# Two transformer blocks on one core: the second block's context norm and 24 context merge gates are computed among the expert pairs

## The reference

```python
def expert_choice_ffn(h, w_router, w_gate, w_up, w_down):
    cap = CAPACITY_FACTOR * n // N_EXPERTS            # 64 tokens for each of 16 experts
    aff = jax.nn.softmax((h @ w_router).astype(jnp.float32), axis=-1)
    gate, idx = lax.top_k(jnp.swapaxes(aff, 1, 2), cap)
    xe = h[bidx, idx]
    hid = jax.nn.silu(xe @ w_gate) * (xe @ w_up)      # per expert, 1024 x 1024 each
    ye = (hid @ w_down) * gate[..., None]
    return jnp.zeros_like(h).at[bidx, idx].add(ye)

def trunk_layer(x, xc, mod, mod_c, ..., with_ctx_out):      # second block
    z = split_columns_2((rmsnorm(x, pre_g) * (1 + scale) + shift) @ w_in)
    zc = split_columns_2((rmsnorm(xc, pre_g) * (1 + scale_c) + shift_c) @ w_in)
    ...
def merge_branches(zz, y_mla, y_pool, y_gla, w_bm, w_bp, w_bg, w_out):
    gates = jax.nn.sigmoid(zz['merge'])               # 3 x 1024 columns
    g_mla, g_pool, g_gla = jnp.split(gates, N_BRANCH, axis=-1)
    merged = g_mla * (y_mla @ w_bm) + g_pool * (y_pool @ w_bp) + g_gla * (y_gla @ w_bg)
    return merged @ w_out
```

## Time and profile before

| | |
|---|---|
| median of 3 runs | 2923.61 us (2909.93, 2923.61, 2923.92) |
| profiled execution, its own time | 2912.22 us |
| its span | 2910.3 us |
| PE busy | 2761.8 us (95%), 15104 matmuls |
| PEld busy | 2087.5 us (72%) |
| DVE, ACT, POOL busy | 1032.6, 911.5, 629.2 us |
| weights on SP's queue (q1) | 378.56 MB |
| mean granted TensorE clock | 0.981 |

### The profile page before, as it was taken

How to read it: one execution, slowest core, us unless ns; L and a number is a source line. 1 busy time by engine, 2 the same in 40 slices (tenths; PEclk the granted TensorE clock), 3 DMA queues, 4 the chain that set the end, 5 groups by cost and what they waited for, 6 DMA issues and landing times.

```text
span 2910.3 us, 36846 instructions
## 1 busy us (share of the span) xinstructions
PE 2761.8 (95%) x15104; PEld 2087.5 (72%) x15104; DVE 1032.6 (35%) x1485; ACT 911.5 (31%) x1379; POOL 629.2 (22%) x301
## 2 busy tenths in 40 slices
PE   6999899999989999999999999999998999898998
PEld 4856777788744433337899867999997878676886
DVE  3435512511351111113168443411135066645114
ACT  5222434422331111103333544311124243443223
POOL 1202021144410000001221102322222232105443
PEclk9999999999999999998999899999998999999999
DMA  6244032022369999994121202111123122103222
GB/s 259 73 175 180 1 132 87 30 102 96 136 277 420 422 422 422 422 422 194 62 90 59 80 1 95 59 62 69 58 102 131 58 103 85 44 27 112 101 87 101
DMA packets 65758, 426.19 MB, mean 146 GB/s; under 512 B 6928, under 2 KB 6928, under 8 KB 19280
## 3 DMA queue, kind: packets, MB, share of 16 engines
q1 hardware_dynamic: 52992, 378.56, 33.1%
q0 software_dynamic: 3664, 24.60, 2.2%
q10 hardware_dynamic: 8960, 20.97, 2.1%
HBM read 405.49 MB, written 17.04 MB: 145 GB/s over the span
## 4 chain that ended last, share of the span: by engine, by line
PE 77%; DMA 9%; DVE 6%; ACT 4%; issue 2%; POOL 1%; SPq 0%; ACTq 0%; DVEq 0%; POOLq 0%
PE psum L713 74%; DMA ring<-in_weights 5%; PE psum L716 4%; DMA late_slots<-in_weights 3%; DVE small L2362 1%; ACT arena L1824 1%; POOL weight_parts L3086 1%; ACT arena L1802 1%; ACT weight_parts L1748 0%; DVE arena L2825 0%; DVE hidden L2318 0%; DMA saved_residual<-residual 0%; DMA arena<-in_t_count 0%; DMA residual<-in_acts 0%; DVE hidden_low L2314 0%
## 5 line engine op out<-in xcount | busy, mean ns | idle before, releaser
L713 PE MATMUL psum<-hidden_high,weight_parts 128*128 128x384 f32 (+2 forms) x3296 | 863.7, 362 | 24.8 <-issue 7.3
L3086 POOL TENSOR_TENSOR weight_parts<-ring,weight_parts 128x1024 fp32r<-128x1024 f32 x224 | 559.7, 2500 | 1290.9 <-ACT weight_parts L1748 1290.8
L713 PEld LDWEIGHTS psum<-hidden_high,weight_parts 128*128 128x128 f32 x3296 | 601.2, 189 | 98.1 <-issue 17.3
L713 PE MATMUL psum<-hidden_low,weight_parts 128*128 128x384 f32 (+2 forms) x2160 | 650.9, 361 | 1.3 <-DVE merged_low L2430 0.7
L1748 ACT ACTIVATE weight_parts<-ring 128x1024 fp32r<-128x1024 f32 x224 | 236.9, 1059 | 1025.3 <-PE psum L713 989.2
L713 PE MATMUL psum<-arena 128*64 128x128 f32 (+8 forms) x2992 | 451.5, 359 | 11.7 <-DMA arena<-in_weights 6.5
L713 PEld LDWEIGHTS psum<-hidden_low,weight_parts 128*128 128x128 f32 x2160 | 399.6, 189 | 44.2 <-issue 2.5
L713 PEld LDWEIGHTS psum<-arena 128*64 128x64 f32 (+3 forms) x2992 | 255.4, 156 | 167.7 <-issue 129.3
L1802 ACT ACTIVATE arena<-psum 128x512 f32<-128x512 f32 (+2 forms) x202 | 147.8, 739 | 360.3 <-PE psum L713 341.7
L713 PE MATMUL psum<-arena_parts,weight_parts 128*128 128x512 f32 (+2 forms) x1140 | 250.4, 377 | 0.5 <-ACT arena L1802 0.5
L713 PEld LDWEIGHTS psum<-arena_parts,weight_parts 128*128 128x128 f32 x1140 | 211.0, 192 | 32.2 <-ACT arena L1802 0.9
(11 more groups left out here) (315 smaller groups left out, 2436.3 us busy)
## 6 DMA issues: line engine op xcount, KB each, us to landing
ring<-in_weights SPq DMA_DIRECT2D x260, 1024.0 KB, 6.7
late_slots<-in_weights SPq DMA_DIRECT2D x48, 1024.0 KB, 15.2
arena<-in_weights SPq DMA_DIRECT2D x48, 1024.0 KB, 17.3
spilled_projections<-arena ACTq DMA_DIRECT2D x14, 384.0 KB, 2.3
arena<-spilled_projections ACTq DMA_DIRECT2D x3, 1536.0 KB, 12.0
residual<-in_acts SPq DMA_DIRECT2D x4, 768.0 KB, 8.3
arena<-in_bias POOLq DMA_DIRECT2D x1, 3072.0 KB, 10.9
arena<-in_t_count POOLq DMA_DIRECT2D x2, 1536.0 KB, 10.5
```

What stands on the lines that cost most here:

```text
L713: return nc.tensor.matmul(o, lhsT, rhs, start=start, stop=stop)
L3086: G_.tensor_tensor(parts[:, i % 2, 1, :], tile_at(t), parts[:, i % 2, 0, :], ALU.subtract).then_inc(*E.sig("tile_split"))
```

## The change

The loop over pairs is replaced by eight pairs written out on PE, ACT and DVE. The context's sum of squares is taken in pair 0 after `exp_gate`, its root on ScalarE, its spreading on PE before `exp_down`, and its scaling, shift and parting (256 columns, 8 feature tiles) beside `exp_down` of pair 0. Pair 0 has no combine products. After `exp_down` of each of the pairs 0 to 5 stand four context gates: their tiles are 24 more tiles of the stream (12 units), each with a copy on ScalarE into `cHigh`, a subtraction in place on GpSimd, 24 matmuls of 256 columns, a sigmoid into one of three staging areas, and a transfer of 128 KB to memory from ScalarE's queue. In `merge` of layer 0 the gate tiles are still loaded and parted, but multiplied with the image only (24 matmuls of 512 columns); the context's gates come back from memory by a transfer that ScalarE starts after each sigmoid. The norm after the pairs covers the image only. `eHot` moves to the image half of `Hlo`, and SP's last loads into the eight slots follow the new count.

```diff
+CONTEXT_GATES = [(b, g) for f in range(0, KT, 2) for b in range(3) for g in (f, f + 1)]
+GATES_PER_PAIR = 4
...
+        for b, g in context_gates_after(j):
+            c0 = B2["merge"] + b * D + g * P
+            out.append((("cgate", b, g), "w_in_2", (0,), None, np.arange(c0, c0 + P)))
...
-    e1 = e0 + PAIRS * 3 * KT
+    e1 = e0 + PAIRS * 3 * KT + len(CONTEXT_GATES) // 2
...
-                        project_tile(("gate", *tags, b, g), ("gate", key, b, g), chunks)
+                        project_tile(("gate", *tags, b, g), ("gate", key, b, g), IMG)
...
+            def context_gate(b, g):
...
+                hi, lo = split(cHigh[i % 2], a=KT), split(tile_parts(n), a=KT)
+                pe.wait_ge(*E.next("context_weight_high"))
+                ps = group("cgate", b, g)
+                for k in range(KT):
+                    for m, h in enumerate((Hhi, Hlo)):
+                        ins = mm(ps[:, 0:CTX], hi[:, k, :], h[:, k, 0:CTX], k == 0 and m == 0, False)
...
+                pe.wait_ge(*E.next("context_weight_low"))
+                for k in range(KT):
+                    ins = mm(ps[:, 0:CTX], lo[:, k, :], Hhi[:, k, 0:CTX], False, k == KT - 1)
...
-                    if e and k:
+                    if j and e and k:
...
+                expert_product(tag, "exp_gate", j, eXE, after=combine_step)
+                if j == 0:
                     pe.wait_ge(*E.next("context_squares", KT))
                     ps = group("stat", "context")
...
+                if j == 0:
+                    pe.wait_ge(*E.next("context_parted", KT))
+                for b, g in context_gates_after(j):
+                    context_gate(b, g)
...
-            with pe.Fori(0, turns) as it:
...
-            pair("last", PAIRS - 1, PAIRS - 1, None)
+            for j in range(PAIRS):
+                pair(j)
...
-            spread(("pre", 0), 0, range(TT))
+            spread(("pre", 0), 0, range(2, TT))
...
+            def context_high(i):
+
+                n = context_tiles[i]
+                act.wait_ge(*arrived(n))
+                if i >= 2:
+                    act.wait_ge(*E.written("cgate", *CONTEXT_GATES[i - 2]))
+                act_(cHigh[i % 2], tile_at(n), ACT.Copy).then_inc(*E.sig("context_weight_high"))
+
+            def context_gate(i):
+
+                s = i % 3
+                if i >= 3:
+                    act.wait_ge(sem(f"context_spilled{s}"), 16 * (i // 3))
+                evac(("cgate", *CONTEXT_GATES[i]), cStage[s], n=CTX, func=ACT.Sigmoid)
+                act.wait_ge(*E.taken("cgate", *CONTEXT_GATES[i]))
+                act.dma_start(dram["context_gates"][i, :, :], cStage[s]).then_inc(sem(f"context_spilled{s}"), 16)
...
+                        evac(("gate", key, b, g), mSG[:, s, CTX:TOK], IMG, func=ACT.Sigmoid)
+                        if chunks is ALL:
+                            act.dma_start(mSG[:, s, 0:CTX], dram["context_gates"][CONTEXT_GATES.index((b, g)), :, :])\
+                                .then_inc(sem(f"context_gate{s}"), 16)
...
+                for i in gates[0:2]:
+                    context_high(i)
                 act.wait_ge(*E.next("gate_set"))
                 act.wait_ge(*E.written(tag, "exp_down"))
                 act_(eYhi, cols(tag, "exp_down"), ACT.Copy, scale=eGate).then_inc(*E.sig("expert_high"))
...
+                for i in gates:
+                    if i + 2 in gates:
+                        context_high(i + 2)
+                    context_gate(i)
...
-                shift_in(modB[l], 0, ALL)
+                shift_in(modB[l], 0, IMG if l == 0 else ALL)
...
+                            if chunks is ALL:
+                                dve.wait_ge(*E.next(f"context_gate{gate_slot(f, b, g)}", 16))
...
+            for i, n in enumerate(context_tiles):
+                pool.wait_ge(*E.next("context_weight_high"))
+                G_.tensor_tensor(tile_parts(n), tile_at(n), cHigh[i % 2], ALU.subtract)\
+                    .then_inc(*E.sig("context_weight_low"))
```

More of the change, by code:

```diff
@@ L1369, in pair @@
                         add_up(ps, k, cSq, range(2), C("ones")[:, 0:1])
+                expert_product(tag, "exp_up", j, eXE)
+                if not last:
+                    pe.wait_ge(*E.next("selected"))
+                    gather(tag, eSel)
                 pe.wait_ge(*E.next("expert_hidden"))
@@ L1411, in _ @@
             pe.wait_ge(*E.taken("first", "XT"))
-            while state["g"] % 3:
-                ps = group("pad", state["g"])
-                ins = mm(ps[:, 0:2], C("ident"), C("ident")[:, 0:2], True, True)
-                ins.then_inc(psum_full, 1)
-            assert state["owed"] == 1 and state["tile"] % 2 == 0, state
-            assert state["ended"] == state["tile"]
-            turns = PAIRS - 1
-            with pe.Fori(0, turns) as it:
-                E.begin(it, {"groups": 6, "slot": 2, "ring": 16 * 24 // (NSLOT + EXTRA), "expert_hidden": 1,
-                             "combined": 8, "hidden_first": 1, "selected": 1})
-                pair("loop", 0, it, it + 1)
-                assert state["owed"] == 1
-                E.end(turns)
-            state["g"] += 6 * (turns - 1)
-            state["tile"] += 48 * (turns - 1)
-            state["ended"] = state["tile"]
-            pair("last", PAIRS - 1, PAIRS - 1, None)
+            for j in range(PAIRS):
+                pair(j)
             keep_warm(5)
-            pe.wait_ge(*E.taken("last", "exp_down"))
+            pe.wait_ge(*E.taken(("pair", PAIRS - 1), "exp_down"))
             for q in range(4):
@@ L2061, in _ @@
                 act_(cSq[:, k, :], R3[:, k, 0:CTX], ACT.Square).then_inc(*E.sig("context_squares"))
-            pair("last", None)
+            for j in range(PAIRS):
+                pair(j)
+            for s in range(3):
+                act.wait_ge(sem(f"context_spilled{s}"), 16 * (len(CONTEXT_GATES) // 3))
             for k in range(KT):
@@ L2717, in pair @@
                     .then_inc(*E.read(tag, "exp_up"))
-                if not following:
-                    dve.wait_ge(*E.written("stat", "context"))
-                    ts_(var[:, 0:2], cols("stat", "context")[:, 0:2], 1.0 / D, EPS, ALU.mult, ALU.add)\
-                        .then_inc(*E.read("stat", "context"))
                 dve.wait_ge(*E.next("hidden_turned"))
@@ L2731, in pair @@
                     .then_inc(*E.read(tag, "exp_down"))
-                if following:
+                if not last:
                     dve.wait_ge(*E.taken(tag, "exp_down"))
                     set_gates()
-            with dve.Fori(0, PAIRS - 1) as it:
-                E.begin(it, {"groups": 6, "slot": 2, "combine_product": 8, "hidden_turned": 1, "gates_ready": 1,
-                             "expert_high": 1})
-                pair("loop", True)
-                E.end(PAIRS - 1)
-            pair("last", False)
+            for j in range(PAIRS):
+                pair(j)
             dve.wait_ge(*E.upto("combined", E.made["combined"]))
```

184 lines of the change are left out of this document (121 added, 63 removed).

## The result

The changed kernel takes 2881.72 us (median of four executions, 2879.22 to 2888.74), the kernel before 2917.26 (four, 2909.93 to 2923.92). The ratio is 0.9885, 95% interval 0.9863 to 0.9908. By the ratio that is 33.5 us less (27 to 40 by its interval), by the medians 35.5, where 33.2 were forecast, and it is 2881.7 us where 2884 were. The profiled execution is the slowest of the four: 2888.74 us (its span is 2886.9), which is 23.5 us under the profiled one of before.

What follows compares the result with a forecast made beforehand. Transfers and TensorE were taken as close limits in the pairs, TensorE alone in layer 0's merge. Terms: -69.1 + 38.6 - 2.7 = -33.2 us, 2879.0 for the profiled execution; predicted 2884 us, range 2868 to 2908.

Steps and rivals of the forecast that it cites:

- The merge: Merge of layer 0: 24 gate tiles go from 8.32 to 5.44 us each, 69.1 us less.
- The gates on TensorE: Context gates among the pairs: 0.120 us per 256-column matmul, 11.8 us per pair, bounds 10.6 and 16.9.
- The pairs' end: End of the expert pairs: TensorE alone 1367.8 us, transfers alone 1369.6; taken as 1370, pairs 38.6 us longer.
- A spill: Writing a context gate to memory during the pairs: 8.4 us for 24, bounds 0 and 0.87 us each.
- Parts ready in time: Gates behind the pairs: copies and subtractions finish before TensorE wants them, the fourth by 0.7 us; cost 0.
- The rival in which gates wait for their parts: Gates behind six pairs: GpSimd's 2.40 us uncovered twice each, 28.8 us on TensorE's time, 2911 us total; chance 10%.
- Pair 0 and the written-out program: First pair: 6.0 us less without zero combine products, 4.5 more for context sums, 1.5 for slow clock, 0.5 for spreading.
- The starving rival: Written-out pairs: 20 instruction packets from full DMA engines stall TensorE 3 us each, 60 us, 2944 us total; chance 5%.
- The norm: Norm after the pairs: first products about 1.3 us apart instead of 1.91, set by ScalarE; 2.7 us less, bounds 1 to 5.
- The sum: Whole kernel: merge, pairs and norm together 33.2 us less on the profiled execution, 2879.0 us; 2884 us predicted.

Runs made afterwards that it cites:

- e2: Changed kernel with twelve context gates moved, two behind each of pairs 0 to 5, the rest in the merge; pairs' length 489.7 us, ratio 0.9932.
- e3: Changed kernel with the same 24 gates, three behind each of all eight pairs; pairs' length 504.7 us, ratio 0.9908.
- e6: Changed kernel without the product of weights' high part and activations' low part, 16 matmuls a moved gate for 24; pairs' length 508.0 us, ratio 0.9905.
- e5: Changed kernel writing only the first three gates to memory, the merge reading these for all others; pairs' length 507.2 us, ratio 0.9867.
- e9: Changed kernel with three gates behind each of eight pairs and only the first three gates written to memory; pairs' length 499.3 us, ratio 0.9856.
- e4: Changed kernel with each gate's 128 KB written to memory twice; pairs' length 514.7 us, ratio 0.9911.
- e7: Changed kernel with eight extra GpSimd subtractions of 128 columns ahead of each context gate's own; pairs' length 588.8 us, ratio 1.0154.
- e1: Changed kernel with none of the 24 context gates moved, the merge making all gates for both parts; pairs' length 470.2 us, ratio 0.9989.
- e11: e8 run again beside a repeat of the changed kernel on the same chip; pairs' length 504.2 us, 2879.56 us in all, ratio 0.9868.
- e8: Changed kernel with three gates taken from the pairs to replace TensorE's unused matmuls around the last norm; pairs' length 503.6 us, ratio 0.9869.

## Why the prediction was right, point by point

**The merge** (-69.1): -69.2. It came out to 0.1 us, since layer 1 showed the very same tile form. If the copies back cost anything, it is within that.

**The gates on TensorE** (0.120 us a matmul, 11.8 us a pair): the gates are 2.82 to 2.83 us apart, 0.118 a matmul, and a pair takes 66.2 us for 66.6. The line through two measured forms was 2% off. The rule of the Trainium skill's "TensorE: Matmul & The Clock Gate" (section on the measured gap of 56 ns), 0.109 for this form, was 8% off: the measurement decides.

**The pairs' end** (507.5 us from the first matmul, 1370 from 862.5): 508.6. Both limits bind, as said: TensorE in pairs 1 to 6 (no wait for weights, 66.2 us apart), transfers in the last, which takes 55.4 us where TensorE alone was put at 50.4. e2, e3 and e6 show which of the two the sum hangs on: 12 gates move it by 19 us, which is their bytes, and the 3.6 us that TensorE gained in e6 were given back in the last pair but for 0.6. A saving of bytes does not always count in full, as the next point says.

**A spill** (0.35 us, bounds 0 and 0.87): its bytes are worth 0.31. What it costs is between 0.07 (1.4 us for 21, e5) and 0.26 (e9, and 0.25 in e4), by whether the queue would have stood still. So the term of 8.4 us for 24 was too large, and a spill has no fixed price. That the eight slots "cover a few us either way" was too little said: they also stop the queue.

**Parts ready in time** (cost 0): right, but the reason was partly wrong. The step "ScalarE copies the first two tiles before the expert's high part, while `exp_down` runs (about 13.9 us" fails: the tiles land 4.8 us before its end, since the queue is only just in time. The fourth tile's margin was forecast at 0.7 us and is 0.5; its table load takes 1.28 us again and the next activation starts 1.29 us after it, so the 2.66 us of the Trainium skill's "ScalarE: Activation LUTs" (What ACT_TABLE_LOAD costs) are not seen here. The rival in which gates wait for their parts was called 29 us at its worst and given 10%; e7 shows that it is steeper, 80 us for 4.2 more microseconds of GpSimd per tile, and e6 that the margin goes with gates 0.9 us shorter. A cost of 0 hung on these 0.5 us, and the head start of the first two tiles was a third of the one assumed: there was some luck in it.

**Pair 0 and the written-out program**: the 6 us of removed zero products gave nothing in the end (e1), since transfers set the length there; in the sum they stood on TensorE's side alone, which was right. The starving rival is out: 20 packets of instructions in the pairs, as many as were forecast for TensorE alone, and no gap. The Trainium skill's "Runtime: NRT & Kernel Launch" (Instruction fetch mechanics) says that code in a row is fetched ahead. The trace agrees in that TensorE waits for none of these packets, under a DMA share of 1.01.

**The norm** (-2.7, bounds 1 to 5): -1.8, within the bounds but by another limit. TensorE's timeline of the changed kernel there, which answers to the earlier trace rows:

```profile
1395.76 4.05 PE L747 MATMUL psum<-consts_sb 128*128 128x256 f32 x18
1399.46 0.70 PE L747 MATMUL psum<-hidden_high,weight_parts 128*128 128x384 f32 x2
1399.99 0.51 PE L747 MATMUL psum<-hidden_low,weight_parts 128*128 128x384 f32 x2
...
1401.04 0.51 PE L747 MATMUL psum<-hidden_low,weight_parts 128*128 128x384 f32 x2
```

The products were expected 1.3 us apart, behind ScalarE. They start only when the matmuls of no use are over, by when the norm's first tiles are done, and then come 1.05 us apart without a wait. The limit that the prediction named, ScalarE's 1.3 us per tile, is there (its steps start 1.29 us apart) but is hidden behind those matmuls, which were not in its sum. In the stretch around it the granted clock is 0.80 (1379 to 1413), before it was 0.86 (1338 to 1374).

**The sum**: -33.2 forecast. The three terms that it is made of measured -69.2 + 39.5 - 1.8 = -31.5; the later start of the pairs and the rest of layer 0 add 1.8, layer 1 6.4, and that gives -23.3, for -23.4 between the two spans. By the ratio it is -33.5, with 7 us to either side, so that the agreement to 0.3 us is luck; the agreement of the terms, to 1.0 us each, is not.

## What to carry to other kernels

Where two limits lie close together, work out both and take the later one pair by pair; then ask of each saving which limit it is on. Work that is moved into another stage costs what that stage is short of: here bytes, 1.6 us a gate, and not the 2.8 us of matmuls. A transfer has its full price only while the ring has room; where the consumer is slow and the slots are full, the queue stands still, and evening out the demand (three gates instead of four) is what makes a saving of bytes count. An experiment that takes work from one engine has to be read for what the engine waits for next: e6 took 22.6 us from TensorE, and 3.6 came through. And a tile that must go through two more engines before use needs its head start counted from its landing, not from its place in the program.

## What the runs showed of the hardware

- fp32r matmuls of 256 columns start every 0.118 us at a granted clock of 1.00 (2.4 GHz), and every 0.21 us at 0.50 (1.2 GHz), where TensorE came from the small matmuls of the statistics: a gate is 2.83 us, and the first late gate 4.85 (e11) and 5.3 (e8).
- The granted clock of one stretch of layer 1 was 0.98 in one execution and 0.88 in another with no change in its code, 4 us for 70. A comparison of two profiles has to be read stage by stage for that.
- 20 packets of instructions were fetched beside weights at 420 GB/s, and TensorE waited for none of them.
- A table load of ScalarE lasts 1.28 us and the next activation starts 1.29 us after it started (990.33, 991.62).
